# A float32 transformer trunk with split weights: GpSimd's weight split in four quarters

## What is computed

```python
c_act = silu(c)
for l in range(2):
    sh1, sc1, g1, sh2, sc2, g2 = split(c_act @ ada_w[l] + ada_b[l], 6)
    h = rms_norm(x, norm_mix_g[l]) * (1 + sc1) + sh1
    y = even_mixer(h, ...) if l % 2 == 0 else odd_mixer(h, ...)
    x = x + g1 * y
    h = rms_norm(x, norm_ffn_g[l]) * (1 + sc2) + sh2
    x = x + g2 * ((silu(h @ w_gate[l]) * (h @ w_up[l])) @ w_down[l])
```

## Time and profile before

| | us |
|---|---|
| median of 3 runs | 3007.84 (3003.31 to 3010.27) |
| span of the profiled execution | 3004.5 |
| TensorE busy | 2681.0 (89%) |
| VectorE busy | 1770.1 (59%) |
| ScalarE busy | 476.0 (16%) |
| GpSimd busy | 711.7 (24%) |

### The profile page before, as it was taken

The page is one execution under the profiler, slowest core; times in us unless marked ns, Lnnn a source line. Parts: engine busy times, 40 slices in busy tenths (PEclk is TensorE's granted clock), DMA queues, the critical chain, the costliest instruction groups (busy, mean ns, idle before and its releaser), DMA issues. The chain is left out here.

```text
span 3004.5 us, 34243 instructions
## 1 busy us (share of the span) xinstructions
PE 2681.0 (89%) x11394; PEld 2143.1 (71%) x11394; DVE 1770.1 (59%) x2882; ACT 476.0 (16%) x847; POOL 711.7 (24%) x404
## 2 busy tenths in 40 slices
PE   2898888699999999999688888887789999999998
PEld 2686666577777777777466666665568888888786
DVE  5758778657555554555857777778566333343332
ACT  2000111110000000000134444444110000000001
POOL 1122112222222222333021111112032233323320
PEclk7899999799999999999789999996799999999998
DMA  6343223502222222222210000001311111111101
GB/s 210 105 121 110 84 84 91 168 15 71 70 70 70 77 70 87 73 77 77 77 32 29 29 28 29 28 28 49 123 43 43 42 42 51 54 49 42 56 28 56
DMA packets 278364, 201.87 MB, mean 67 GB/s; under 512 B 5994, under 2 KB 247812, under 8 KB 278148
## 3 DMA queue, kind: packets, MB, share of 16 engines
q1 hardware_dynamic: 262996, 159.94, 17.9%
q10 hardware_dynamic: 15280, 40.90, 3.6%
HBM read 179.84 MB, written 20.97 MB: 67 GB/s over the span
## 5 line engine op out<-in xcount | busy, mean ns | idle before, releaser
L506 PE MATMUL psG<-h_hi,w_split 128*128 128x512 f32 x2496 | 1007.6, 404 | 73.4 <-DVE h_lo L1105 35.1
L511 PE MATMUL psG<-h_lo,w_split 128*128 128x512 f32 x2496 | 990.3, 397 | 0.0
L512 PE MATMUL psG<-h_hi,w_split 128*128 128x512 f32 x2496 | 988.4, 396 | 0.0
L486 POOL TENSOR_SCALAR w_split<-w_raw 128x1024 fp32r<-128x1024 f32 x200 | 225.9, 1129 | 2188.6 <-PE psG L506 878.1
L506 PEld LDWEIGHTS psG<-h_hi,w_split 128*128 128x128 f32 x2496 | 480.3, 192 | 200.8 <-issue 46.6
L512 PEld LDWEIGHTS psG<-h_hi,w_split 128*128 128x128 f32 x2496 | 479.2, 192 | 102.5
L511 PEld LDWEIGHTS psG<-h_lo,w_split 128*128 128x128 f32 x2496 | 480.2, 192 | 98.4 <-issue 3.3
L488 POOL TENSOR_TENSOR w_split<-w_raw,w_split 128x1024 fp32r<-128x1024 f32 x200 | 486.7, 2434 | 16.7
L1374 DVE TENSOR_TENSOR hid<-sil,psG 128x512 f32<-128x512 f32 x88 | 60.5, 687 | 601.2 <-PE psG L512 601.1
L1384 DVE SCALAR_TENSOR_TENSOR xT<-psG,mod,xT 128x512 f32<-128x512 f32 x352 | 257.0, 748 | 153.6 <-PE psG L512 153.3
L506 PE MATMUL psG<-hid_hi,w_split 128*128 128x512 f32 x704 | 283.2, 402 | 30.3 <-DVE xT L1384 27.0
(11 more groups left out here) (142 smaller groups left out, 2297.5 us busy)
## 6 DMA issues: line engine op xcount, KB each, us to landing
ada_raw<-in_ada_w SPq DMA_DIRECT2D x80, 512.0 KB, 4.0
w_raw<-in_ffn_w_gate SPq DMA_DIRECT2D x44, 512.0 KB, 3.8
w_raw<-in_ffn_w_up SPq DMA_DIRECT2D x44, 512.0 KB, 3.8
w_raw<-in_ffn_w_down SPq DMA_DIRECT2D x44, 512.0 KB, 4.2
w_raw<-in_ev_w_in SPq DMA_DIRECT2D x28, 512.0 KB, 5.5
w_raw<-in_od_w_qkv SPq DMA_DIRECT2D x24, 512.0 KB, 3.6
ada_first<-in_ada_w SPq DMA_DIRECT2D x4, 2048.0 KB, 12.9
x_spill<-xT ACTq DMA_DIRECT2D x2, 4096.0 KB, 11.7
```

The lines of the kernel that those rows point to most:

```text
L486: nc.gpsimd.tensor_scalar(slot[:, 0], raw[:], 1.0, 1.0, ALU.mult, ALU.mult).then_inc(hi_done, 1)
L506: mm = nc.tensor.matmul(o, st[0], mv[0], start=first, stop=False, **kw)
L511: nc.tensor.matmul(o, st[0], mv[1], start=False, stop=False, **kw)
L512: return nc.tensor.matmul(o, st[1], mv[0], start=False, stop=end, **kw)
```

## The change

GpSimd's two instructions over a slab become eight over 256 columns each: first four multiplications (high part), then four subtractions (low part). Each of the first four raises `hi_done`; the subtraction of quarter q waits for `4 n + q + 1`, which is its own quarter's high part. The first three subtractions raise a new semaphore `lo_part`, for which nothing waits, the last one `slab_ready` as before. SyncE, TensorE, VectorE and ScalarE are unchanged, and the numbers computed are the same.

```diff
+QUARTERS = 4
...
+        lo_part = sem("lo_part")
...
                         pool.sem_inc(pool_turn, 1)
-                        nc.gpsimd.tensor_scalar(slot[:, 0], raw[:], 1.0, 1.0, ALU.mult, ALU.mult).then_inc(hi_done, 1)
-                        pool.wait_ge(hi_done, n + 1)
-                        nc.gpsimd.tensor_tensor(slot[:, 1], raw[:], slot[:, 0].bitcast(F32), ALU.subtract).then_inc(slab_ready, 1)
+                        for q in range(QUARTERS):
+                            part = slice(q * D // QUARTERS, (q + 1) * D // QUARTERS)
+                            nc.gpsimd.tensor_scalar(slot[:, 0, part], raw[:, part], 1.0, 1.0, ALU.mult, ALU.mult).then_inc(hi_done, 1)
+                        for q in range(QUARTERS):
+                            part = slice(q * D // QUARTERS, (q + 1) * D // QUARTERS)
+                            pool.wait_ge(hi_done, QUARTERS * n + (q + 1))
+                            lo = nc.gpsimd.tensor_tensor(slot[:, 1, part], raw[:, part], slot[:, 0, part].bitcast(F32), ALU.subtract)
+                            lo.then_inc(slab_ready if q == QUARTERS - 1 else lo_part, 1)
```

## The result

The changed kernel takes 2930.4 us (median of 4 runs, 2928.0 to 2935.4) against 3007.1 us of the kernel before on the same chip: ratio 0.975, interval 0.973 to 0.977. The forecast was 2946 us, 16 us more; the time lies in the stated range.

The account below looks back on a forecast made before the run. TensorE was taken to bound most of the span, idling where VectorE, held by GpSimd, is late. 67 us gained less 5 us cost takes 3004.5 to 2942.5, plus 3.3 us for the median: 2946 us, range 2895 to 3020.

Parts of the forecast that it names:

- The mechanism: VectorE and GpSimd shut each other out for whole instructions where both read SBUF; VectorE can go between quarters.
- Quarters of 480 and 820 ns: GpSimd's quarter copies and subtractions last 0.48 and 0.82 us; a slab takes 5.2 us for 3.45.
- 1.25 us gained a slab, 53.5 slabs, 67 us: VectorE's loss falls from 2.85 to 1.6 us a slab; 53.5 slabs' loss reaches TensorE: 67 us.
- Costs of 5 us: Two slabs that TensorE already waits for are each ready some 2.5 us later: 5 us.
- up to 15 us more: TensorE's clock, outside the sum: fewer gaps could give up to 15 us more.
- The two long gaps in the heads: TensorE's 2.7 and 3.0 us gaps in the heads fall to 1 to 2 us, a head 3 us shorter.
- 0.8 slab a chunk: Feed-forward 0: 0.8 slab a chunk reaches TensorE, with 4 for the ends, 11 slabs.
- the 4 slabs: Behind the two norms after the projections, slabs meet the norm's chain, much absorbed by queued matmuls: 4 slabs together.
- More is freed: Rival, chance 0.12: VectorE meets quarters by chance only, loses 0.7 us a slab; 2898 us.
- the same total: Rival, chance 0.08: VectorE waits out every piece, 2.87 us a slab, no gain; 3008 to 3013 us.
- The pair isn't given up between quarters: Rival, chance 0.06: the shared port pair stays held across quarters, above all in the copies; 3008 to 3013 us.
- Slower: Rival, chance 0.12: each quarter holds a fixed part, at 0.1 us a piece VectorE loses 3.7 us a slab; 3056 us.

Follow-up runs that it names:

- e5: Kernel before, whole instructions kept, with six extra 16-column GpSimd subtractions between each slab's copy and subtraction; 3002.9 us, ratio 0.9987.
- e4: Changed kernel with only the copy (high part) in quarters, the subtraction left whole; 2967.4 us, ratio 0.987 to the kernel before.
- e2: Changed kernel with eight pieces of 128 columns in place of four of 256; 2938.2 us, ratio 0.977 to the kernel before.
- e1: Changed kernel with two pieces of 512 columns in place of four of 256; 2969.8 us, ratio 0.988 to the kernel before.

## Why the prediction was right

**The mechanism and its size.** The mechanism holds for quarters: no VectorE instruction of this trace is held across two whole quarters, and VectorE's busy time falls by 168.4 us. Whole, in halves, in quarters and in eighths it is busy 1770.1, 1674.5, 1601.7 and 1579.8 us; in retention and heads it falls with each step, in the middle of feed-forward 0 it rises again from quarters to eighths. e5 shows that later slabs alone don't give the gain of the whole kernel, but not that place plays no part in a single stage. Sizes, by the prediction's steps:
- Quarters of 480 and 820 ns: 486 and 813 measured in the mean, but with what they wait for VectorE; half of them take no more than 411 and 745 ns, so that the estimate of a bare one was some 70 ns too long; GpSimd busy 982 us for some 1050. GpSimd's part of the slab, unheld, is 1.52 + 2.82 = 4.34 us for a forecast 5.2, since pieces overlap by a tenth of a microsecond each.
- 1.25 us gained a slab, 53.5 slabs, 67 us: this is the term that was too large. TensorE's idle time fell by 48.8 us net of 3.2 us of new waits for GpSimd: 52.0 / 53.5 = 0.97 us. In the heads VectorE's busy time fell by 25.2 us over 214 / 8 = 27 slabs, 0.94 each. The value was chosen between 0.7 and 2.87 of loss, nearer to the busy case; VectorE loses 1.9 us a slab, a little nearer to every piece being waited out.
- Costs of 5 us: the two waits for GpSimd went from 2.83 and 1.55 to 4.09 and 3.48 us, 3.2 us together:

```profile
130.67 0.72 PE L513 MATMUL psG<-h_hi,w_split 128*128 128x512 f32 x1 [4.09 <-POOL w_split L494]
...
696.00 0.47 PE L513 MATMUL psG<-hid_hi,w_split 128*128 128x512 f32 x1 [3.48 <-POOL w_split L494]
```

- The clock, left out of the sum with "up to 15 us more": 22.9 us. Stretches with a granted clock of 0.5, which is 1.2 GHz, add up to 397 us of the span before and 321 after. Set against the forecast span of 2942.5: 62 - 48.8 = 13.2 us too much of idle time saved, 22.9 us of clock not counted, 9.7 us left, which is 2942.5 - 2932.8. The two errors cancel in part, and the forecast's nearness owes that much to luck. The other 5.7 us of the distance from 2945.8 is that the median here lies 2.4 us below the profiled span and not 3.3 above.

**Where the stages went as forecast.** Retention 16.1 us for 15, start 4.5 for 2.5, output projection 0 4.1 for 4. The heads' window gave 28.5 us for 27 (17.5 slabs in the heads and 4 beside the last one, x 1.25), but of these 19.8 are idle time, and the forecast was for idle time alone; 8.7 are clock. The two long gaps in the heads became (timeline of after):

```profile
1619.67 0.69 PE L724 MATMUL psM<-s_sq,consts 128*128 128x512 f32 x1 [0.90 <-ACT s_sq L838]
...
1639.52 0.73 PE L761 MATMUL psZ<-s_sum,split_c 128*128 128x512 f32 x2 [1.07 <-DVE s_sum L1470]
```

0.90 and 1.07 us, for a forecast 1 to 2, and no gap over 1.4 us behind s_sum is left. From the long wait on s_sq of one head to that of the next is 76.0 us before and 72.6 after (mean of five), 3.4 us less, for 3. Retention's wait for r_v is 1.95 to 2.37 us in three of the four heads, for 2; in the first it is still 4.38 us.

**Where they didn't.** Feed-forward 0 was to give 11 slabs, 9 us of it in the nine middle chunks at 0.8 slab each. They are 3.3 us longer. The step that failed is the 0.8 slab a chunk; that the slabs, "spread over a longer time", "hit nearer to the point that counts" was seen and priced too low. The timeline of a chunk of after:

```profile
764.70 3.46 POOL L494 TENSOR_TENSOR w_split<-w_raw,w_split 128x256 fp32r<-128x256 f32 x4
...
764.68 0.69 DVE L1381 TENSOR_TENSOR hid<-sil,psG 128x512 f32<-128x512 f32 x1 [4.10 <-PE psG L519]
765.40 1.03 DVE L1110 CAST hid_hi<-hid 128x512 fp32r<-128x512 f32 x1
766.46 1.10 DVE L1112 TENSOR_TENSOR hid_lo<-hid,hid_hi 128x512 fp32r<-128x512 f32 x1
...
768.28 3.46 DVE L1125 SCALAR_TENSOR_TENSOR ada_acc<-ada_raw,c_act,ada_acc 128x128 f32<-128x128 f32 x7
...
772.54 0.79 PE L513 MATMUL psG<-hid_hi,w_split 128*128 128x512 f32 x1 [2.46 <-DVE xT L1391]
```

VectorE had waited 4.10 us for hid's product: whatever it had been spared earlier in the chunk was spent here. From 764.68 on, the cast and the subtraction meet quarters (1.03 and 1.10 us for 0.43 and 0.69), the adaLN steps ahead of xT, which had taken their bare 2.68 us before (796.65), take 3.46 us, and TensorE stands for 2.46 us, much what it stood before (31.2 us in 13). In this chunk a saving would have helped only behind the last point at which VectorE waits for TensorE; the prediction counted slabs, not that.

Feed-forward 1 was to stay, and its stage, with norm 3 ahead of it, got 11.8 us shorter. For norm 3 the prediction had a share of the 4 slabs, 5 us, that it gave to both norms behind the projections; norm 1's stage alone got 6.1 us shorter. Waits of TensorE on norm 3's h_lo in the first 95 us of the stage, before:

```profile
PE psG L506 <- DVE h_lo L1176: 7.0, 4, 2.9
```

and after:

```profile
PE psG L513 <- DVE h_lo L1183: 1.0, 1, 1.0
```

That is 6 us of idle time; the other 6 are busy time (734.1 us for 740.3). Before, a stretch of 13.7 us at 1.2 GHz stood at this norm; after, none does.

**The rivals.** "More is freed" and "the same total" are out by the sizes above. "The pair isn't given up between quarters" falls for quarters by the 1.10 us among the subtractions and by the copies of e4; for pieces of 128 columns it is what happened in 25 places of e2, in feed-forward 0 and the norms. "Slower", a fixed part in each piece of over 0.15 us, is out for quarters by the time, and e2 speaks against such a part in retention and heads, where VectorE's busy time falls again with 16 pieces a slab, by 14.6 us in the heads. The 115 ns that the prediction takes from the Trainium skill's page ("SBUF — State Buffer", "A bandwidth-pool intuition that's wrong (but worth ruling out)") stand there for GpSimd going on, with a DMA's descriptors, behind a VectorE instruction. VectorE's busy time can't show a cost on GpSimd's side, and no run here separates it.

## What to carry over

Where GpSimd and VectorE both read SBUF, a long GpSimd instruction is a long delay of VectorE, so it is to be cut where VectorE is on the chain. Cut it no finer than the trace bears out: with 256 columns everywhere no VectorE instruction was held across two whole pieces, with 128 one instruction of 0.35 us waited out eight of them (3.27 us). The number of pieces is to be chosen stage by stage: here 8 in the attention stages and 2 in conv and feed-forward 0 gave 120 us where 4 everywhere gave 77. Count a saving only if it lies behind the last point where the engine that is freed waits for something else, and read the stage, not the mean of a form. A cut also moves the later slabs, and that alone moved stages by up to 12 us here (e5). Price TensorE's idle gaps with the clock that follows them: here 22.9 us of busy time went with 48.8 us of idle time.

## What was not expected of the hardware

- **Cost of a narrow GpSimd instruction.** From 1.05 and 2.36 us at 1024 columns and 0.38 and 0.705 us each back to back at 256, a copy costs 0.16 us and 0.87 ns a column, a subtraction 0.15 us and 2.16 ns a column. So the price of a cut is some 0.16 us of GpSimd's time, and not the 0.3 us by which the prediction had each piece longer than its share.
- **The first cuts pay unevenly.** In the heads VectorE's busy time fell by 3.4 us from whole to halves, 21.8 from halves to quarters, 14.6 from quarters to eighths. The heads as a whole even took 605.0 us with halves, more than the 599.6 of before, though TensorE's idle time fell. Window of e1:

```profile
1498.60:2103.60 605.00, 520.36 (x2107) 394.05 (x2105) 449.39 (x861) 279.95 (x539) 118.28 (x107) 0.88 0.10 32
```

84.6 us idle for 91.9, but the same matmuls busy for 520.4 us and not 507.7, at a mean granted clock of 0.88 and not 0.90. Why more of this stage ran at 1.2 GHz with less idle time stays open.
